# Second block's forgetting attention: VectorE evicts the projection half and makes the weights' low parts ahead of scaling the probabilities

## The chip, the cores and the metric

The kernel runs on one NeuronCore of one Trainium2 chip. The core has five engines that run side by side, each on its own list of instructions in order: TensorE (PE), VectorE (DVE), ScalarE (ACT), GpSimd (POOL) and SyncE (SP), and they wait for each other by semaphores. The metric is the time of one execution on the device in microseconds (us); the kernel before and the changed one are compared by the medians of their runs.

## The reference, cut to what matters

Two blocks of two layers each work on 512 tokens of 1024 features in float32. The change touches the attention of the second block alone, which is computed once in each of its two layers ("the two passes"):

```python
def forgetting_attention(q, k, v, logf):          # (1, 8 heads, 512, 64)
    c = jnp.cumsum(logf, axis=-1)
    for i in range(S // Q_BLOCK):                  # 4 blocks of 128 queries
        logits = einsum(q_block, k[:q1]) * HEAD_DIM_2 ** -0.5
        logits = logits + (c[q0:q1, None] - c[None, :q1])
        p = softmax(where(causal, logits, -inf))
        outs.append(einsum(p, v[:q1]))
```

In the same layer the input is projected by a wide matrix (`h @ w_in[l]`) to queries, keys, values, convolution inputs, pooling input and gates, most of which the attention doesn't need. After the attention come the convolution, pooling and gated merge, an output projection and a gated feed-forward part.

## The kernel before, in words

**Projections.** Weights arrive from HBM in units of 128x2048 float32. The matmuls want them as two rounded parts: ACT writes the high part (`split` in the scalar block: `wH<-raw`, L1298), DVE subtracts it from the raw unit and writes the low part (`split` in the vector block: `wL<-raw,wH`, L1755). Each product is then three passes over the array (L472). There are two buffers for units. A job is one group of matmuls into one of two slots of the PSUM tensor `G`. DVE frees the slot by reading it out (an eviction), and counts that in `job_free`; PE starts a job only when the one two before it was freed.

**The attention loop.** 8 heads by 4 query blocks give 32 rows; two rows (one query block of a pair of heads) are a step d, with d from 0 to 15, and the row's width is 128, 256, 384 or 512 keys in turn. Every engine has the same loop over d written out by hand in its own block of the program, so the order of each engine is the order of its code:

- PE (L1175 to L1212), step d: scores of rows 2d and 2d+1 into `psS` (L1157), a quarter of a projection unit (`fill(2d)`), the transposes of rows 2d-2 and 2d-1 into `psT` (L1193; they wait for `p_ready`), a second quarter (`fill(2d+1)`), and from step 2 on the product of two rows' probabilities with the values (L1166, `pv_pair`). `fill(13)`, in step 6, ends with sums of squares of the queries (L531, 16 small matmuls) which go into the PSUM bank `G[:, 1, :]`. That bank also holds the first finished attention output, so L531 waits for `pv_free`, which DVE's first `heads_out` counts.
- ACT (L1692 to L1706), step d: the exponential of rows 2d and 2d+1 (L1405, `p_exp`), the copies of the transposed rows 2d-2 and 2d-1 (L1411), in steps 6, 10 and 14 its half of `heads_out` (L1689), and in `fill(2d)` of every even step the high part of a weight unit (L1298). In step 14 it also rounds the pooling branch (L1682, L1683).
- DVE (L2680 to L2698), step d: scale and mask the scores and take the row maximum, for rows 2d and 2d+1 (`row`: L2556, L2559, L1997); then the reciprocal of the sums (L2690) and the scaling of the probabilities (L2691, which counts `p_ready`); in steps 6, 10 and 14 `heads_out` (L2639, which counts `pv_free`); then `fill(2d)`, which evicts the half job of the step before (L2578, L2580, L2587, L2593, in two steps after L2598 for the keys) and in every even step makes the low part of a unit (L1755); then `fill(2d+1)`, which holds pieces of the pooling branch (L2648 to L2668).

The rows' probabilities lie in four buffers by row number, the sums and reciprocals in four columns.

Of the kernel before, what the change touches and what calls it, by code (L numbers as in the profile page):

```python
# [211 lines left out]
def program(nc, a, out, scratch):  # L212
    ctx = contextlib.ExitStack()
    with ctx:
# [1532 lines left out]
        def _(dve):  # L1747
# [3 lines left out]
            def split():  # L1751

                g = c.unit
                dve.wait_ge(wh_ready, g.v + 1)
                V.tensor_tensor(wL[:, g.p, :], raw[:, g.p, :], wH[:, g.p, :].bitcast(F32), ALU.subtract)\  # L1755
                    .then_inc(wl_ready, 1)
                g.off += 1
# [87 lines left out]
            def rstd_part(at):  # L1845

                c.sq.off += 1
                dve.wait_ge(sq_used, c.sq.v)
                over = rb2[:, 0:8].unsqueeze(1).to_broadcast([P, 2, 8])
                c.link(V.tensor_tensor(ms[:, 0:16].rearrange("p (n c) -> p n c", n=2),  # L1850
                                       at[:, 0:16].rearrange("p (n c) -> p n c", n=2), over, ALU.mult))
                V.tensor_scalar(ms[:, 0:16], ms[:, 0:16], 1.0 / 64, EPS, ALU.mult, ALU.add).then_inc(ms_ready, 1)
                c.stat.off += 1

            def rstd_part_scaled(dst):

                dve.wait_ge(rs_ready, c.stat.v)
                d = dst.rearrange("p (n c) -> p n c", n=2)
                c.link(V.tensor_tensor(d, d, rbc[:, 0:8].unsqueeze(1).to_broadcast([P, 2, 8]), ALU.mult))
# [27 lines left out]
            def column_pairs(first):  # L1887

                wait(dve, rb_ready, c.bc.v - 1)
                V.tensor_copy(wide[:, c.bc.p, :].rearrange("p (n c) -> p n c", c=64),  # L1890
                              rsb[:, first:first + 8].unsqueeze(2).to_broadcast([P, 8, 64])).then_inc(cols_ready, 1)
                c.bc.off += 1
# [103 lines left out]
            def row_max(r, src):  # L1996
                return V.tensor_reduce(mxt[:, r % 4:r % 4 + 1], src, AX.X, ALU.max, negate=True)  # L1997
# [140 lines left out]
            for l in range(2):  # L2138
                if l == 0:
# [165 lines left out]
                    for lev in range(7):  # L2305
                        for h in range(4):
# [7 lines left out]
                            if lev < 6:  # L2314
                                if lev == 0:
                                    b = psS[:, n % 2, :].rearrange("p (k q) -> p k q", q=P)
                                    d = ws[:, DD + h, :].rearrange("p (k q) -> p k q", q=P)
                                    ins = V.tensor_tensor(d, b, hmask[:, 0:1, :].to_broadcast([P, 4, P]), ALU.mult)
                                else:
# [4 lines left out]
                                    d = later(ws[:, DD + h, :].rearrange("p (k q) -> p k q", q=P))  # L2324
# [15 lines left out]
                else:  # L2340
# [30 lines left out]
                    def row(r):  # L2371
                        h, qt = r // ST, r % ST
                        c.link(V.scalar_tensor_tensor(probs(r), psS[:, r % 2, 0:(qt + 1) * P], rsq[:, r:r + 1],
                                                      ws[:, OE + h, (3 - qt) * P:S], ALU.mult, ALU.add))
                        row_max(r, probs(r)).then_inc(mx_ready, 1)
# [137 lines left out]
            for l in c.layers(2, chain=CHAIN_2, **LAYER):  # L2513
# [56 lines left out]
                def half_raw(t, dst, mul=None):  # L2570

                    if t == 0:
                        dve.wait_ge(act_read, c.ar.v + 1)
                        c.ar.off += 1
                    else:
                        dve.wait_ge(sq_ready, c.sq.v + 1)
                    if mul is None:
                        half(lambda g: V.tensor_copy(dst, g), unit=(t == 1))  # L2578
                    else:
                        half(lambda g: V.tensor_scalar(dst, g, mul, None, ALU.mult), unit=(t == 1))  # L2580

                def half_values(t):

                    def read(g):
                        for i in range(2):
                            tt = 2 * t + i
                            ins = V.tensor_scalar(ws[:, FV + tt, 256:512], g[:, i * 256:i * 256 + 256],  # L2587
                                                  rbc[:, tt * 2:tt * 2 + 1], None, ALU.mult)
                        return ins
                    half(read, unit=(t == 1))  # L2590

                def half_scaled(t, dst):
                    half(lambda g: V.tensor_tensor(ws[:, dst + t, :], g, rbt, ALU.mult), unit=(t == 1))  # L2593

                def half_keys(t):
                    k_ = ws[:, FK + 2 + t, :]
                    dve.wait_ge(rb_ready, c.bc.v)
                    V.tensor_tensor(k_, k_, G[:, 3, :], ALU.mult).then_inc(kn_read, 1)  # L2598

                def fill(s_):  # L2600

                    if s_ == 2:
                        half_raw(0, ws[:, FK + 2, :])
                    elif s_ == 4:
                        half_raw(1, ws[:, FK + 3, :])
                    elif s_ == 6:
                        rstd_part(G[:, 3, :])
                        half_raw(0, ws[:, FQ + 2, :], gqk[:, 5:6])
                    elif s_ == 8:
                        rstd_part_scaled(rsb[:, 0:16])  # L2610
                        column_pairs(0)
                        half_raw(1, ws[:, FQ + 3, :], gqk[:, 5:6])
                    elif s_ == 10:
                        half_keys(0)
                        half_scaled(0, PX_)
                        column_pairs(8)
                    elif s_ == 12:
                        half_keys(1)
                        half_scaled(1, PX_)
                    elif s_ == 15:  # L2620
                        rstd_part_scaled(rsq[:, 16:32])
                    elif s_ in (17, 19, 21, 23, 25, 27):
                        pooled((s_ - 17) // 2)
                    elif s_ in (14, 16):
                        half_values((s_ - 14) // 2)
                    elif s_ in (18, 20):
                        half_scaled((s_ - 18) // 2, CX)
                    elif s_ in (22, 24):
                        half_scaled((s_ - 22) // 2, CB)
                    elif s_ in (26, 28):  # L2630
                        half_scaled((s_ - 26) // 2, CC)
                    elif s_ in (30, 32, 34, 36):
                        n = (s_ - 30) // 2
                        half_scaled(n % 2, GATE + n // 2 * 2)
# [16 lines left out]
                def pooled(n):  # L2651

                    if n == 0:
                        dve.wait_ge(pinv_in, (c.lay.v - 2) * 16)
                        window(pa, u, 1)
                    elif n == 1:
                        window(pb, pa, 2)
                    elif n == 2:
                        window(pa[:, 1:2, :], pb[:, 1:2, :], 4)
                    elif n == 3:  # L2660
                        window(pb[:, 1:2, :], pa[:, 1:2, :], 8)
                    else:
                        t, rows, widths = ((pa, lo, (2, 8)), (pb, hi, (4, 16)))[n - 4]
                        start = t[rows, :, 0:16]
                        c.link(V.tensor_tensor(start, start, ws[rows, PINV:PINV + 2, 0:16], ALU.mult))
                        V.tensor_tensor(start, start, u[rows, :, 0:16], ALU.subtract)
                        for i, width in enumerate(widths):
                            ins = V.scalar_tensor_tensor(t[rows, i, 16:S], t[rows, i, 16:S], 1.0 / width, u[rows, i, 16:S],  # L2668
                                                         ALU.mult, ALU.subtract)
                        ins.then_inc(pd_ready, 1)  # L2670
# [9 lines left out]
                for d in range(16 + 3):  # L2680
                    if d == 7:
                        rstd_part(G[:, 1, :])
                    if d < 16:
                        for r in (2 * d, 2 * d + 1):
                            dve.wait_ge(s_done, c.row.v + (r + 1))
                            row(r)
                    if d < 16:
                        for r in (2 * d, 2 * d + 1):
                            dve.wait_ge(p_exp, c.row.v + (r + 1))
                            c.link(V.reciprocal(rden[:, r % 4:r % 4 + 1], den[:, r % 4:r % 4 + 1]))  # L2690
                            V.tensor_scalar(probs(r), probs(r), rden[:, r % 4:r % 4 + 1], None, ALU.mult)\  # L2691
                                .then_inc(p_ready, 1)
                    if d in (6, 10, 14):
                        heads_out((d - 6) // 4)
                    fill(2 * d)
                    if d == 0:
                        split()
                    fill(2 * d + 1)  # L2698
                heads_out(3)
# [266 lines left out]
```

## Time and profile before

| | us |
|---|---|
| median of 3 runs (lowest to highest) | 3091.82 (3090.43 to 3093.57) |
| the profiled execution | 3094.84 |
| its span, first to last instruction | 3093.1 |
| PE busy in the span | 3076.0 (99%) |
| DVE, ACT, POOL busy | 1568.6 (51%), 1091.7 (35%), 236.9 (8%) |
| first pass of the attention loop | 1665.90 to 1806.30 |
| second pass | 2399.00 to 2540.00 |

The span is what the instructions cover; the profiled execution has 1.7 us around it. "Busy" counts an engine's instructions as they overlap on it. In a timeline the times are us from the start of the span, and the brackets at the end of a row give how long the engine sat idle before the instruction and which instruction released it. PE overlaps its matmuls, so that two of them that lie 0.23 us apart each show some 0.39 us.

### The profile page before, as it was taken

To read this page: it belongs to the slowest core of one execution; us is meant where nothing else is said; L and a number is where in the kernel's file an instruction comes from. 1 tells how busy PE (TensorE), PEld (TensorE's weight loads), DVE (VectorE), ACT (ScalarE), POOL (GpSimd) and SP (SyncE) were. 2 spreads that over 40 slices of the span, in tenths; PEclk is the share of its full clock that TensorE was granted. 3 is DMA by queue.
4 is the path that set the end of the run, shared out by engine and by line. 5 is a ranking of instruction groups with operands and counts; after the bars stand their busy time and mean duration, and the time that the engine had idled before them with its cause. 6 is when DMAs were issued, how large, how long until landed. Compare 5 with 4: busy or idle time off the path is not lost.

```text
span 3093.1 us, 36907 instructions
## 1 busy us (share of the span) xinstructions
PE 3076.0 (99%) x15434; PEld 2577.6 (83%) x15434; DVE 1568.6 (51%) x1887; ACT 1091.7 (35%) x1175; POOL 236.9 (8%) x138
## 2 busy tenths in 40 slices
PE   9999999999999999999999999999999999999999
PEld 8798988888889798888888778888888878888887
DVE  7564555554335654555436764544334766443432
ACT  3223344443223433444323332334322342333321
POOL 0002100010000010001001000101100000100100
PEclk9999999999999999999999999999999999999999
DMA  4412312223322131222333122222233223223222
GB/s 172 116 55 82 136 55 95 95 95 109 113 105 96 55 137 55 96 107 83 109 109 103 69 96 96 96 95 95 95 109 115 74 79 106 87 94 108 89 102 95
DMA packets 47758, 299.82 MB, mean 97 GB/s; under 512 B 7107, under 2 KB 7395, under 8 KB 13460
## 3 DMA queue, kind: packets, MB, share of 16 engines
q1 hardware_dynamic: 43376, 285.94, 26.2%
q10 hardware_dynamic: 4260, 12.10, 1.6%
q8 instruction: 95, 1.56, 0.2%
q14 instruction: 27, 0.22, 0.0%
HBM read 293.26 MB, written 4.77 MB: 96 GB/s over the span
## 4 chain that ended last, share of the span: by engine, by line
PE 93%; DVE 4%; ACT 2%; issue 1%; POOL 0%; DMA 0%; SPq 0%; DVEq 0%; ACTq 0%
PE G L472 86%; DVE wL L1755 1%; PE psS L830 1%; DVE mxt L1997 1%; ACT wH L1298 1%; PE psS L528 1%; PE psS L1029 1%; PE psS L1157 1%; PE G L1166 0%; PE G L1036 0%; PE G L991 0%; DVE ws L2556 0%; PE psT L1193 0%; PE psS L961 0%; PE psT L560 0%
## 5 line engine op out<-in xcount | busy, mean ns | idle before, releaser
L472 PE MATMUL G<-hH,wH 128*128 128x512 f32 x2560 | 1015.9, 397 | 6.5 <-DVE ws L2593 1.9
L472 PE MATMUL G<-hH,wL 128*128 128x512 f32 x2560 | 999.6, 390 | 0.0
L472 PE MATMUL G<-hL,wH 128*128 128x512 f32 x2560 | 998.5, 390 | 0.0
L1755 DVE TENSOR_TENSOR wL<-raw,wH 128x2048 fp32r<-128x2048 f32 x258 | 621.9, 2410 | 485.5 <-ACT wH L1298 485.4
L1298 ACT ACTIVATE wH<-raw 128x2048 fp32r<-128x2048 f32 x261 | 498.8, 1911 | 775.5 <-PE G L472 757.5
L472 PE MATMUL G<-wsr,wH 128*128 128x512 f32 (+1 forms) x2496 | 739.3, 380 | 2.4 <-DVE wsr L2389 1.9
L472 PEld LDWEIGHTS G<-hH,wH 128*128 128x128 f32 x2560 | 481.9, 188 | 119.2 <-issue 18.7
L472 PEld LDWEIGHTS G<-hH,wL 128*128 128x128 f32 x2560 | 481.4, 188 | 102.1
L472 PEld LDWEIGHTS G<-hL,wH 128*128 128x128 f32 x2560 | 482.2, 188 | 98.6 <-issue 1.2
L472 PEld LDWEIGHTS G<-wsr,wH 128*128 128x128 f32 x2496 | 459.8, 188 | 92.7 <-DVE wsr L2389 2.8
L472 PE MATMUL G<-wsr,wL 128*128 128x512 f32 (+1 forms) x1248 | 472.5, 379 | 0.0
L472 PEld LDWEIGHTS G<-wsr,wL 128*128 128x128 f32 x1248 | 234.9, 188 | 43.5
L2815 POOL TENSOR_TENSOR wsr<-sq,wsr 128x1024 f32 x44 | 105.9, 2406 | 836.5 <-ACT wsr L1436 836.5
L1878 DVE TENSOR_TENSOR sq<-G,hmask 128x1024 f32<-128x1024 f32 x44 | 53.9, 1225 | 217.6 <-PE G L472 217.6
L1436 ACT ACTIVATE wsr<-sq 128x1024 f32 x44 | 46.7, 1060 | 309.9 <-DVE sq L2020 309.9
L1405 ACT ACTIVATE ws<-ws,mxt 128x128 f32<-128x128 f32 (+3 forms) x96 | 54.0, 563 | 188.6 <-DVE mxt L1997 188.0
L1930 DVE TENSOR_TENSOR x<-x,G 128x1024 f32<-128x1024 f32 x38 | 46.4, 1221 | 142.0 <-PE G L472 142.0
L2793 POOL TENSOR_TENSOR rsb<-ms,neghalf 128x4 f32<-128x4 f32 (+4 forms) x20 | 36.8, 1842 | 998.6 <-DVE ms L1809 859.3
L472 PE MATMUL G<-wH,hH 128*128 128x256 f32 x384 | 112.2, 292 | 0.3 <-DVE ws L2381 0.3
L472 PE MATMUL G<-wH,hL 128*128 128x256 f32 x384 | 108.6, 283 | 0.0
L472 PE MATMUL G<-wL,hH 128*128 128x256 f32 x384 | 108.6, 283 | 0.0
L1878 DVE TENSOR_TENSOR tn<-G,hmask 128x1024 f32<-128x1024 f32 x44 | 53.9, 1225 | 95.2 <-PE G L472 94.8
(306 smaller groups left out, 2533.1 us busy)
## 6 DMA issues: line engine op xcount, KB each, us to landing
raw<-in_units SPq DMA_DIRECT2D x263, 1024.0 KB, 4.8
ws<-bias_rows SPq DMA_DIRECT2D x2, 1536.0 KB, 15.2
bias_rows<-ws ACTq DMA_DIRECT2D x1, 2560.0 KB
x<-in_x SPq DMA_DIRECT2D x4, 512.0 KB, 7.6
ws<-in_mem ACTq DMA_DIRECT2D x2, 1024.0 KB, 4.7
ws<-bias_rows ACTq DMA_DIRECT2D x1, 2048.0 KB, 8.6
ws<-norm_rows ACTq DMA_DIRECT2D x1, 2048.0 KB, 7.0
out_x<-x SPq DMA_DIRECT2D x3, 512.0 KB, 7.2
```

The lines of the kernel that those rows point to most:

```text
L472: mm = pe.matmul(o, mv if swap else wt, wt if swap else mv, start=first and n == 0, stop=last and n == 2)
L528: mm = pe.matmul(st[:, col:col + 1], lhs, ones[:, 0:1], start=True, stop=True)
L830: mm = pe.matmul(psS[:, n % 2, o:o + w], k_[:, ks:ks + P], q, start=True, stop=True)
L1029: mm = pe.matmul(psS[:, r % 2, 0:M], ws[:, XQ + 2 * h + t, qt * P:qt * P + P], kx[:, 2 * h + t, :], start=(t == 0), stop=(t == 1))
L1298: activation(wH[:, g.p, :], raw[:, g.p, :], ACT.Copy).then_inc(wh_ready, 1)
L1405: return activation(p_, p_, ACT.Exp, bias=mxt[:, r % 4:r % 4 + 1], accum_out=den[:, r % 4:r % 4 + 1])
L1436: activation(aH[:, bass.ds(i * 2, 2), :], sq[:, 1], ACT.Copy).then_inc(ffn_h, 1)
L1755: V.tensor_tensor(wL[:, g.p, :], raw[:, g.p, :], wH[:, g.p, :].bitcast(F32), ALU.subtract)\
L1878: V.tensor_tensor(dst, g, rb_pair, ALU.mult).then_inc(job_free, 1)
L1930: V.tensor_tensor(x[:, 2 * jj:2 * jj + 2, :], x[:, 2 * jj:2 * jj + 2, :], g, ALU.add)\
L2793: W.tensor_tensor(dst[:, at:at + cols], ms[:, at:at + cols], neghalf[:].to_broadcast([P, cols]), ALU.pow)\
L2815: W.tensor_tensor(aL[:, bass.ds(i * 2, 2), :], sq[:, 1], aH[:, bass.ds(i * 2, 2), :].bitcast(F32), ALU.subtract).then_inc(ffn_ready, 1)
```

## The change

In each step of the attention loop but the first, DVE's `fill(2d)` now stands ahead of the scaling of the probabilities of rows 2d and 2d+1. All that `fill(2d)` does goes with it: the eviction of the half job, in the even steps the low part of a weight unit (L1755) with its wait for ACT's high part, and in steps 6 and 12 and the like whatever else that index holds. `heads_out` of steps 6, 10 and 14 stood between the two and now comes after both. Step 0 keeps its order.

```diff
@@ -2684,6 +2684,8 @@
                         for r in (2 * d, 2 * d + 1):
                             dve.wait_ge(s_done, c.row.v + (r + 1))
                             row(r)
+                    if d:
+                        fill(2 * d)
                     if d < 16:
                         for r in (2 * d, 2 * d + 1):
                             dve.wait_ge(p_exp, c.row.v + (r + 1))
@@ -2692,8 +2694,8 @@
                                 .then_inc(p_ready, 1)
                     if d in (6, 10, 14):
                         heads_out((d - 6) // 4)
-                    fill(2 * d)
                     if d == 0:
+                        fill(0)
                         split()
                     fill(2 * d + 1)
                 heads_out(3)
```

The scaling has lines 2692 and 2693 in the changed file. DVE's order in step 6, from the end of `row(13)` to the start of step 7, before (in brackets the semaphores that a row waits for):

```order
L2690 RECIPROCAL rden<-den 128x1 [waits p_exp]
L2691 TENSOR_SCALAR ws<-ws,rden 128x384 [waits dve_chain]
L2690 RECIPROCAL rden<-den 128x1 [waits p_exp]
L2691 TENSOR_SCALAR ws<-ws,rden 128x384 [waits dve_chain]
L2639 TENSOR_TENSOR wsr<-G,wsr 128x512 [waits pvh_ready,pv_done]
L2598 TENSOR_TENSOR ws<-ws,G 128x512 [waits rb_ready]
L2593 TENSOR_TENSOR ws<-G,hmask 128x512 [waits job_done]
L1755 TENSOR_TENSOR wL<-raw,wH 128x2048 [waits wh_ready]
L1850 TENSOR_TENSOR ms<-G,rb 128x16 [waits sq_used]
```

and now:

```order
L2598 TENSOR_TENSOR ws<-ws,G 128x512 [waits rb_ready]
L2593 TENSOR_TENSOR ws<-G,hmask 128x512 [waits job_done]
L1755 TENSOR_TENSOR wL<-raw,wH 128x2048 [waits wh_ready]
L2692 RECIPROCAL rden<-den 128x1 [waits p_exp]
L2693 TENSOR_SCALAR ws<-ws,rden 128x384 [waits dve_chain]
L2692 RECIPROCAL rden<-den 128x1 [waits p_exp]
L2693 TENSOR_SCALAR ws<-ws,rden 128x384 [waits dve_chain]
L2639 TENSOR_TENSOR wsr<-G,wsr 128x512 [waits pvh_ready,pv_done]
L1850 TENSOR_TENSOR ms<-G,rb 128x16 [waits sq_used]
```

`heads_out` (L2639) and the two scalings now stand behind the low part (L1755), which waits for ACT's high part. Steps 10 and 14 have the same pattern; in step 10 the half of the keys is not there and a pooling piece follows. Before:

```order
L2691 TENSOR_SCALAR ws<-ws,rden 128x384 [waits dve_chain]
L2690 RECIPROCAL rden<-den 128x1 [waits p_exp]
L2691 TENSOR_SCALAR ws<-ws,rden 128x384 [waits dve_chain]
L2639 TENSOR_TENSOR wsr<-G,wsr 128x512 [waits pvh_ready,pv_done]
L2593 TENSOR_TENSOR ws<-G,hmask 128x512 [waits job_done]
L1755 TENSOR_TENSOR wL<-raw,wH 128x2048 [waits wh_ready]
```

and now:

```order
L2593 TENSOR_TENSOR ws<-G,hmask 128x512 [waits job_done]
L1755 TENSOR_TENSOR wL<-raw,wH 128x2048 [waits wh_ready]
L2692 RECIPROCAL rden<-den 128x1 [waits p_exp]
L2693 TENSOR_SCALAR ws<-ws,rden 128x384 [waits dve_chain]
L2692 RECIPROCAL rden<-den 128x1 [waits p_exp]
L2693 TENSOR_SCALAR ws<-ws,rden 128x384 [waits dve_chain]
L2639 TENSOR_TENSOR wsr<-G,wsr 128x512 [waits pvh_ready,pv_done]
```

The orders of PE, ACT, POOL and SP are the same in both kernels.

## Rows read from the trace of the kernel before

**Rows 1.** The page: busy time by engine, share of the span, instructions.
```profile
PE 3076.0 (99%) x15434; PEld 2577.6 (83%) x15434; DVE 1568.6 (51%) x1887; ACT 1091.7 (35%) x1175; POOL 236.9 (8%) x138
```

**Rows 2.** PE's waits, whole span: us in total, times, longest us.
```profile
PE G L472 <- DVE ws L2593: 1.9, 4, 0.7
```

**Rows 3.** PE in the first pass: us, PE busy (x), PEclk, DMA share, GB/s.
```profile
1665.90:1806.30 140.40, 139.47 (x827) 1.00 0.20 72
```

**Rows 4.** Timeline of DVE, first pass, step 6: start us, us, instruction.
```profile
1715.98 0.15 DVE L2690 RECIPROCAL rden<-den 128x1 f32<-128x1 f32 x1
...
1717.04 0.42 DVE L2691 TENSOR_SCALAR ws<-ws,rden 128x384 f32<-128x384 f32 x1
1717.94 0.69 DVE L2639 TENSOR_TENSOR wsr<-G,wsr 128x512 fp32r<-128x512 f32 x1 [0.48 <-ACT wsr L1689]
1718.55 0.68 DVE L2598 TENSOR_TENSOR ws<-ws,G 128x512 f32<-128x512 f32 x1
...
1719.74 2.28 DVE L1755 TENSOR_TENSOR wL<-raw,wH 128x2048 fp32r<-128x2048 f32 x1
1721.94 0.17 DVE L1850 TENSOR_TENSOR ms<-G,rb 128x16 f32<-128x16 f32 x1
```

**Rows 5.** Timeline of ACT, high parts of steps 6, 10 and 14.
```profile
1717.72 1.92 ACT L1298 ACTIVATE wH<-raw 128x2048 fp32r<-128x2048 f32 x1
...
1750.70 1.92 ACT L1298 ACTIVATE wH<-raw 128x2048 fp32r<-128x2048 f32 x1
...
1782.22 1.92 ACT L1298 ACTIVATE wH<-raw 128x2048 fp32r<-128x2048 f32 x1
```

**Rows 6.** Timeline of PE, small matmuls of step 6, first and second pass.
```profile
1719.28 1.84 PE L531 MATMUL G<-halves,sq 128*128 128x2 f32 x16
...
2452.62 1.84 PE L531 MATMUL G<-halves,sq 128*128 128x2 f32 x16
```

**Rows 7.** Timeline of DVE, second pass, `heads_out` of step 6.
```profile
2451.28 0.69 DVE L2639 TENSOR_TENSOR wsr<-G,wsr 128x512 fp32r<-128x512 f32 x1 [0.48 <-ACT wsr L1689]
```

**Rows 8.** Timeline of DVE, first pass, steps 9 to 11.
```profile
1746.07 0.62 DVE L2556 SCALAR_TENSOR_TENSOR ws<-psS,rsq,ws 128x384 f32<-128x384 f32 x1 [0.31 <-PE psS L1157]
...
1752.65 2.29 DVE L1755 TENSOR_TENSOR wL<-raw,wH 128x2048 fp32r<-128x2048 f32 x1 [0.45 <-ACT wH L1298]
1754.87 0.68 DVE L2648 TENSOR_TENSOR sq<-sq 128x508 f32<-128x508 f32 x1
...
1755.79 0.75 DVE L2556 SCALAR_TENSOR_TENSOR ws<-psS,rsq,ws 128x512 f32<-128x512 f32 x1
...
1758.60 0.69 DVE L1997 TENSOR_REDUCE mxt<-ws 128x1 f32<-128x512 f32 x1
```

**Rows 9.** Timeline of PE, first pass, steps 5, 12, 15 and 16.
```profile
1707.46 0.38 PE L1193 MATMUL psT<-ident,ws 128*128 128x128 f32 x2
...
1760.40 0.49 PE L1157 MATMUL psS<-ws 64*128 64x128 f32 x4
...
1761.60 0.47 PE L472 MATMUL G<-hH,wH 128*128 128x512 f32 x1 [0.71 <-DVE ws L2593]
...
1787.83 0.82 PE L1193 MATMUL psT<-ident,ws 128*128 128x128 f32 x6
...
1792.20 0.47 PE L472 MATMUL G<-hH,wH 128*128 128x512 f32 x1 [0.22 <-DVE ws L2593]
```

**Rows 10.** Timeline of DVE, first pass, step 15's first row.
```profile
1786.39 0.74 DVE L2556 SCALAR_TENSOR_TENSOR ws<-psS,rsq,ws 128x512 f32<-128x512 f32 x1
```

**Rows 11.** Timeline of PE, start of the kernel.
```profile
9.76 0.50 PE L472 MATMUL G<-hH,wH 128*128 128x512 f32 x1 [1.82 <-DVE wL L2113]
...
10.32 0.59 PE L472 MATMUL G<-hH,wL 128*128 128x512 f32 x1
...
13.70 0.43 PE L472 MATMUL G<-hL,wH 128*128 128x512 f32 x1
```

**Rows 12.** PE in a window there: us, PE busy (x), PEclk, DMA share, GB/s.
```profile
11.30:13.30 2.00, 2.00 (x7) 0.50 1.06 446
```

## The prediction, made before the changed kernel ran

> **What bounds the kernel now.** I read the page first: PE is busy for 3076.0 us of the span of 3093.1 [rows 1]. So the kernel can be made faster only where PE stands still, and whatever makes PE stand still longer is added to the time in full. Next, PE's own waits: the only ones that DVE's evictions in the attention loop cause are four on L2593, 1.9 us in total [rows 2]. The first pass of the loop shows PE at granted clock 1.00, with 0.93 us of 140.40 not busy [rows 3]. That is the whole prize. Last, the timelines of the two passes, to see how late each step of DVE's could come before PE waits for it. What DVE hands to PE in the loop is p_ready (scaled rows), the row maximum with the emptied score bank, job_free (evictions), wl_ready (low parts) and, once at step 6, pv_free.
>
> **Part 1, the gain.** The four waits are two in each pass, 0.71 us in step 12 and 0.22 us in step 16 of the first [rows 9] and the same in the second. An eviction that comes earlier can end them: at most -1.9 us. In the odd steps the eviction moves ahead of two scalings, 1.1 us or less.
>
> **Part 2, heads_out of step 6.** DVE finishes row 13 at 1715.98 and then before scaled two rows, ran heads_out (L2639) from 1717.94 to 1718.63, evicted, and made the low part [rows 4]. PE's sums of squares, which wait for that heads_out, start at 1719.28 [rows 6]. So heads_out had a slack of 0.6 us. Now it stands behind L1755, and L1755 waits for ACT's high part, which runs from 1717.72 to 1719.64 [rows 5] and isn't moved by the change: ACT's exponentials, copies and its half of heads_out wait for nothing that the change delays before this point. Forward from 1715.98: L2598 and L2593 take 0.60 each from start to start, to 1717.18. L1755 starts 0.03 after the high part, 1719.67, and frees DVE 2.20 later (1719.74 to 1721.94 in rows 4), at 1721.87. The two scalings took 1.48 from 1715.98 to the end of L2691 at 1717.46; 0.25 of it was the wait for the second exponential, which is long over now, and 0.15 of the rest overlaps the next instruction or the first: 1.08 is left, to 1722.95. heads_out takes 0.69, to 1723.64. PE's matmuls, seen at 1719.28, can issue from 1719.16, when the last weights of the quarter have gone in, and now issue at 1723.67. **That is a new stall of 4.5 us.** It lies on PE's own list: scores, quarters and transposes behind it can't pass. DVE starts step 7 with L1850, which waits for just these sums, so DVE, and ACT behind its maxima, shift by the same 4.5 us and nothing is caught up. The second pass has heads_out at 2451.28 and the sums at 2452.62 [rows 6, 7], the same 1.34 us apart: another 4.5. Two passes: +9.0 us.
>
> **Part 3, the scalings behind L1755 in steps 8 to 15** (times without the shift of part 2, which all engines share). In an even step the low part is bound by ACT, so the two scalings, hidden before in DVE's wait for ACT, now follow it and delay the next row. In step 8 that is 0.8 us (128 wide); 0.21 and 0.31 us of idle time in step 9 take part of it back [rows 8], and 0.3 us reach step 10. There: high part to 1752.92 (1750.70 + 1.92 + 0.3) [rows 5], low part to 1755.15, scalings 1.08, heads_out 0.61, the pooling piece 0.92 (1754.87 to 1755.79 [rows 8]): step 11's first row starts at 1757.76 instead of 1755.79, 1.97 us late. Its last maximum ends at 1761.26 instead of 1759.29. PE wants that maximum for the scores of step 12 at 1760.40 [rows 9]: wait 0.9. The eviction behind it ends at 1761.86, and the quarter that before started at 1761.60, after its own wait of 0.71, starts at 1761.89. Net +0.3: the wait that the change aims at isn't ended but replaced. Steps 12 and 13 carry some 1.5 us of lag on to step 14, where the high part ends near 1785.64 instead of 1784.14 [rows 5], the low part at 1787.87, and the second scaling at 1788.99. PE wants it for the transposes at 1787.83 + 0.3 [rows 9]; the first row's three come first, and PE loses 0.5. heads_out follows, and step 15's rows start at 1789.6 instead of 1786.39 [rows 10], its eviction ends near 1793.7, and PE, which before started step 16's quarter at 1792.20 [rows 9], starts it 1.5 us late in all. Part 3: +1.5 a pass, +3.0 us, with part 1 already inside it. Bounds: 0 (if DVE's idle time in steps 11 to 13 takes in more than I count) and 5.0 (2.5 a pass, if every 1.97 us of lag came through at the second place as well).
>
> Before step 6 I count nothing. The lags there are 0.7 to 1.0 us by the same reckoning; the closest is step 4's scaling, which I find ready at 1706.3, where PE's transposes stand at 1707.46 [rows 9], and DVE's wait for the scores of step 6 takes the lag in. PE, ACT and SP get no instruction more. SP's loads wait for L1755, which comes no earlier and at most 2 us later for a unit needed two steps on.
>
> **Part 4, PE's clock after a stall.** The loop has no stall of 4.5 us to read from. The nearest row is the kernel's start: PE idles for 1.82 us to 9.76, and from 10.32 the matmuls stand 0.43 apart instead of 0.23, at granted clock 0.50 in 11.30 to 13.30, that is 1.2 GHz, until 13.70 [rows 11, 12]. Eight steps in 3.38 us instead of 1.82: 1.6 us lost. A hole of 4.5 us, followed by 16 matmuls of two columns, is deeper than that one, while the work before it is denser. I take the fall as likelier than not: +1.6 a pass, +3.2 us. Bounds: 0, and twice that, 6.4 us, since the low clock may hold through the sums as well. The Trainium skill, page "TensorE: Matmul & The Clock Gate", section "Why this matters for your kernels", says that gaps without work between bursts of matmuls put the array back to its lower clock. By that rule the sum is 15.2 us, without it 12.0; the trace agrees at its start, and nowhere else does it show a stall long enough.
>
> **Sum.** 9.0 + 3.0 + 3.2 = +15.2 us. Against the profiled execution, 3094.84, that is 3110.0. It lies 3.0 us above the median of the runs shown, so against the median 3091.82: **3107.0 us** (+0.49%).
>
> **Rivals.** (a) The clock stays at 1.00 through both stalls: +12.0, 3103.8. For it speaks the dense work ahead of the stall, against it rows 11 and 12. (b) The low clock lasts longer, or falls again with the smaller stalls: 9.0 + 3.0 + 6.4 = 18.4, 3110.2. (c) Part 2 holds alone and DVE's idle time takes in the rest: +9.0, 3100.8. (d) Faster: the earlier evictions end the four waits and nothing takes their place, -1.9, 3089.9. The mechanism needs step 6's heads_out done by 1719.16, so ACT's high part would have to be done 4.5 us earlier than at 1719.64, before ACT's copies are; the trace shows nothing that moves it. The Trainium skill, page "Perfetto Trace Analysis", section "Optimization Strategy", advises to find the gaps of the busiest engine and to make what they wait for start sooner. That is this rival; it would give 3089.9, and rows 4 to 6 speak against it because the same move makes a tighter dependency start later. (e) The change does nothing: evictions and scalings swap places and every consumer has slack, 3091.8. It falls by the same 0.6 us of slack.
>
> **Chances.** Forecast 0.55, (a) 0.25, (b) 0.10, (c) 0.05, (e) 0.03, (d) 0.02. A measurement of this kernel can tell about 0.2% (6.2 us) from no change. Forecast and (a) to (c) all lie above 3098.0: slower 0.95, same 0.03, faster 0.02. The range takes in (c) to (b), with the bound of 5.0 of part 3: 3100 to 3112.
>
> **What would show it.** PE's waits after: a new one before L531 of some 4.5 us in each pass, released by DVE's L2639; waits of 0.2 to 1 us before L1157 in step 12 and L1193 in step 15; in step 6, L1755 idle for some 2.5 us before its start and L2693 behind it; the clock below 1.00 in the windows right behind the two stalls. Wrong would be: L531 waiting less than 3 us (another order of ACT's), the passes longer than 149 us (something else late, such as a weight unit), or time added outside the two passes.

## The result, and the profile after

The changed kernel takes 3113.3 us (median of 6 runs, 3110.31 to 3114.28) against 3093.4 us for the kernel before in the same comparison (6 runs, 3090.43 to 3095.32): ratio 1.0062, 95% interval 1.0052 to 1.0072, that is 19 us slower (16 to 22); the two medians lie 19.9 us apart. Forecast were 3107.0 us (+15.2) and a range that ended at 3112. The direction was right, the size was 4.7 us short, and another 1.6 us come from the kernel before, whose median is 3093.4 in this comparison and was 3091.8 in the runs that the forecast started from.

PE's waits in the stretch of the whole span (same view as [rows 2]: us in total, times, longest us):

```profile
PE G L531 <- DVE wsr L2639: 8.5, 2, 4.2
PE G L472 <- DVE ws L2593: 2.0, 4, 0.8
...
PE psS L1157 <- DVE mxt L1997: 1.5, 2, 0.7
...
PE psT L1193 <- DVE ws L2693: 0.6, 2, 0.3
```

The first line is new: two stalls ahead of the sums of squares, released by `heads_out`. The second is the line that the change aims at; in sum it is as large as before, but split in another way: in the first pass step 12's wait fell from 0.71 to 0.20 us and step 16's rose from 0.22 to 0.82 (step 16 is the loop's turn behind the last rows). The third and fourth are new too, the late maxima of step 11 and the late scaling of step 14.

DVE in step 6 of the first pass (it answers to [rows 4]; everything up to here lies 4.4 us earlier than in the profile of before, see below):

```profile
1711.58 0.68 DVE L2598 TENSOR_TENSOR ws<-ws,G 128x512 f32<-128x512 f32 x1
1712.18 0.69 DVE L2593 TENSOR_TENSOR ws<-G,hmask 128x512 f32<-128x512 f32 x1
1715.28 2.29 DVE L1755 TENSOR_TENSOR wL<-raw,wH 128x2048 fp32r<-128x2048 f32 x1 [2.41 <-ACT wH L1298]
1717.49 0.15 DVE L2692 RECIPROCAL rden<-den 128x1 f32<-128x1 f32 x1
...
1718.54 0.68 DVE L2639 TENSOR_TENSOR wsr<-G,wsr 128x512 fp32r<-128x512 f32 x1
1722.89 0.17 DVE L1850 TENSOR_TENSOR ms<-G,rb 128x16 f32<-128x16 f32 x1 [3.67 <-PE G L531]
```

DVE now sits idle for 2.41 us ahead of the low part, with `heads_out` behind it on its own list, and then for 3.67 us while PE does what `heads_out` released. ACT's high part was where it had been (1713.32 to 1715.24, with the same 4.4 us).

PE in the same step, and its granted clock there (second fence: us, PE busy (x), PEclk, DMA share, GB/s), which answer to [rows 6] and [rows 3]:

```profile
1719.28 3.58 PE L531 MATMUL G<-halves,sq 128*128 128x2 f32 x16 [4.24 <-DVE wsr L2639]
1722.78 0.69 PE L1166 MATMUL G<-ws 128*64 128x128 f32 x4
1723.41 2.08 PE L1157 MATMUL psS<-ws 64*128 64x512 f32 x4
```

```profile
1715.00:1719.20 4.20, 0.04 (x1) 0.75 0.17 31
1719.20:1722.60 3.40, 3.32 (x16) 0.50 0.67 275
1722.60:1726.00 3.40, 3.40 (x12) 0.50 0.00 0
1726.00:1729.00 3.00, 3.00 (x22) 0.77 0.00 0
1729.00:1733.00 4.00, 4.00 (x36) 1.00 0.00 0
```

The same 16 matmuls took 1.84 us before [rows 6] and take 3.58, and the four scores behind them take 2.08 instead of 1.13. The clock fell to 0.50 (1.2 GHz) while PE stood still, and was back at 1.00 only some 8 us after it had resumed.

**Where the time went.** One pass, from the first scores (L1157) to the last product with the values (L1166), took 139.27 and 139.31 us before, from start to start, and takes 148.87 and 149.37. Cut at three instructions that both traces show:

| stretch | first pass, us before and after | difference | second pass, difference |
|---|---|---|---|
| step 0's scores to step 6's scores | 46.21, 46.04 | -0.17 | -0.15 |
| step 6's scores to L531 | 7.13, 11.53 | +4.40 | +4.40 |
| L531 to step 7's transposes | 6.17, 9.96 | +3.79 | +4.28 |
| step 7's transposes to the end | 79.76, 81.34 | +1.58 | +1.53 |
| sum | | +9.60 | +10.06 |

The 0.15 us that both passes gain in the first stretch are won in step 5, where the 4 matmuls of L560 start earlier. The two passes together are 19.7 us longer, which is nearly all of the 19.9 between the medians. The profiled execution of the changed kernel, 3110.31 us, is the shortest of its six runs, and only 15.5 above the profile of before. The rest lies ahead of the attention loop, which begins at 1661.71 in it and at 1665.94 before: in the profile of before the clock fell several times for a few us at places the change doesn't touch, the start [rows 12] among them, and here less often. At the start:

```profile
11.30:13.30 2.00, 2.00 (x11) 1.00 1.05 438
```

Such falls are there in one profile and not in another. PE waits 1.9 us on L2389 in both kernels, to 1020.27 us before and to 1017.58 after; the clock fell there before (first line) and not after (second line):

```profile
1018.00:1026.00 8.00, 6.11 (x32) 0.79 0.47 152
1018.00:1026.00 8.00, 8.00 (x51) 1.00 0.69 257
```

I read the steps of 1.5 to 3 us between runs of one kernel as such falls. The granted clocks of the runs fit: of e11's eleven runs below, the five of 3089.7 to 3090.0 us have a mean of 0.999, the six of 3091.5 to 3093.0 one of 0.998. So the passes' lengths are the sharper measure of the stalls below, beside the medians; but each is read from one execution, and the loss to the clock within a pass can differ from one to the next as well.

### The profile page after: what moved, and what is told of

The parts are those of the page before. It is cut to its first block, busy times and chain, and to the rows that moved or that the text cites. A ratio compares the mean times of both kernels' runs of the same rounds, so it can differ in the third digit from the quotient of the medians.

```text
span 3108.5 us, 36907 instructions
## 1 busy us (share of the span) xinstructions
PE 3080.6 (99%) x15434; PEld 2578.6 (83%) x15434; DVE 1565.1 (50%) x1887; ACT 1092.1 (35%) x1175; POOL 237.7 (8%) x138
## 4 chain that ended last, share of the span: by engine, by line
PE 91%; DVE 6%; ACT 2%; issue 1%; POOL 0%; DMA 0%; SPq 0%; DVEq 0%; ACTq 0%
PE G L472 84%; DVE wL L1755 1%; ACT wH L1298 1%; DVE mxt L1997 1%; PE psS L830 1%; PE psS L1029 1%; DVE ws L2556 1%; PE psS L528 1%; PE psS L1157 0%; PE G L1036 0%; PE G L991 0%; PE G L1166 0%; PE psT L560 0%; PE psS L961 0%; PE G L531 0%
## 5 line engine op out<-in xcount | busy, mean ns | idle before, releaser
L1755 DVE TENSOR_TENSOR wL<-raw,wH 128x2048 fp32r<-128x2048 f32 x258 | 621.9, 2411 | 500.6 <-ACT wH L1298 500.5
```

## The experiments

Eleven runs of ten kernels. "Over before" is the difference of the medians in the same comparison; "passes" are the two lengths as above, less those of before.

| run | over before, us | ratio (95% interval) | passes, us |
|---|---|---|---|
| e1, heads_out first | +0.5 | 1.0000 (0.9991 to 1.0010) | +0.2, +0.2 |
| e2, low part last | -1.8 | 0.9996 (0.9986 to 1.0005) | -1.1, -1.2 |
| e3, step 6 alone | +15.6 | 1.0050 (1.0033 to 1.0067) | +9.1, +8.3 |
| e4, all but step 6 | +2.6 | 1.0010 (1.0001 to 1.0020) | +1.4, +1.4 |
| e5, 2 repeats | +1.1 | 1.0004 (0.9995 to 1.0014) | +0.4, +0.3 |
| e6, 4 repeats | +8.5 | 1.0029 (1.0017 to 1.0040) | +3.4, +3.3 |
| e7, 6 repeats | +15.0 | 1.0051 (1.0035 to 1.0068) | +4.8, +6.3 |
| e8, 3 repeats, wait ahead of the quarter | +12.1 | 1.0041 (1.0027 to 1.0055) | +5.5, +7.8 |
| e9, 8 repeats | +16.8 | 1.0054 (1.0039 to 1.0069) | +7.8, +7.9 |
| e10, 4 repeats, wait ahead of the quarter | +12.0 | 1.0041 (1.0026 to 1.0057) | +6.0, +6.2 |
| e11, low part last, again | -1.8 | 0.9993 (0.9984 to 1.0002) | -1.1, -1.1 |

### Which part of the change costs what (e1 to e4)

**e1.** `heads_out` back ahead of `fill(2d)`, against the changed kernel:

```diff
+                    if d in (6, 10, 14):
+                        heads_out((d - 6) // 4)
                     if d:
                         fill(2 * d)
...
-                    if d in (6, 10, 14):
-                        heads_out((d - 6) // 4)
```

> The changed kernel with heads_out moved back, to the place right behind the rows and ahead of fill(2d); the scalings stay behind fill(2d). Theory (heads_out behind the low part makes the stall before L531, 4.2 us a pass in the changed kernel, and the low clock after it, 3.8 us a pass, comes from that stall): both are gone, no wait before L531, clock 1.00 in both passes, and only the waits behind the late scalings are left, 0.6 to 1.6 us a pass: 1 to 3 us over the kernel before. Rival (the lateness of the scalings is what costs, and heads_out only shows it): still 10 us or more over the kernel before.

Measured: +0.5 us over the kernel before, no wait before L531, and of PE's waits in the two passes only these:

```profile
PE G L472 <- DVE ws L2593: 0.8, 4, 0.2
PE psT L1193 <- DVE ws L2695: 0.5, 2, 0.3
```

One line that moves takes away all but half a us of 19. The late scalings cost even less than expected. The wait for the late maxima (L1157) is gone, as it should be if `heads_out` no longer adds its 0.6 us to the lag of steps 10 and 14. The listed waits are 0.6 us less than before in sum (1.9 to 1.3), yet the passes are 0.2 us longer each. So the list doesn't hold all that a late hand-over costs: the six transposes that waited in step 15 now also take 1.07 us in place of 0.82 [rows 9].

**e2.** The evictions ahead of the scalings, but the low part behind them and behind `heads_out`, against the changed kernel (and in `half`, `late.append(1)` for `split()`):

```diff
                     if d in (6, 10, 14):
                         heads_out((d - 6) // 4)
+                    if late:
+                        split()
+                        late.pop()
```

> The changed kernel with the eviction ahead of the scalings as in the change, but the low part of the unit (L1755) behind the scalings and behind heads_out. Theory (what hurts is only the wait for ACT's high part, which stands ahead of the scalings and heads_out): no wait before L531, because heads_out ends 0.3 us later than in the kernel before against a slack of 0.5 to 0.6, and the four waits on L2593 shrink: 0 to 2 us faster than the kernel before. Rival (even the evictions, 0.6 to 1.2 us, are too much ahead of heads_out): a wait before L531 of some tenths of a us to 1 us, and if that is enough to lower the clock, 3 us or more a pass.

Measured: -1.8 us by the medians, both passes 1.15 us shorter. No wait of PE's in either pass is left, neither the four on L2593 nor one of the new kinds. About 1 us of the 1.15 lies behind step 7, where the waits were, and the rest in step 5, for which the prediction counted nothing. The first theory held. So "evict first" was sound; what spoilt it is that `fill(2d)` also holds a wait for ACT.

**e3.** The change in step 6 alone, against the changed kernel:

```diff
-                    if d:
+                    if d == 6:
                         fill(2 * d)
...
                         heads_out((d - 6) // 4)
+                    if d != 6:
+                        fill(2 * d)
                     if d == 0:
-                        fill(0)
```

> The change in step 6 alone, all other steps in the order of before. Theory (the whole cost of step 6 is stall plus low clock, and the late scalings of steps 8 to 15 are a cost of their own): wait before L531 4.2 us, low clock 3.8 us a pass, so 16.0 us over the kernel before. Rival (the low clock needs the late scalings around it, or the other steps cause part of the stall): less than 12 us over.

**e4.** The change in all steps but 6, against the changed kernel:

```diff
-                    if d:
+                    if d not in (0, 6):
                         fill(2 * d)
...
                         heads_out((d - 6) // 4)
+                    if d in (0, 6):
+                        fill(2 * d)
                     if d == 0:
-                        fill(0)
```

> The change in all steps but step 6. Theory: no wait before L531, clock 1.00 in both passes, and the waits of steps 11 to 16 cost 1.5 us a pass: 3.0 us over the kernel before. Rival (those waits are a consequence of the stall of step 6): within 1 us of the kernel before.

e3 gave +15.6 us with 4.24 us of wait before L531 in each pass, e4 +2.6. They add up to 18.2, about the changed kernel's 19.9, and both lie where the theory put them. The clock took 4.7 us of e3's first pass and 3.9 of its second. e4's waits are the two small ones of the changed kernel (same view):

```profile
PE G L472 <- DVE ws L2593: 2.0, 4, 0.8
...
PE psS L1157 <- DVE mxt L1997: 1.5, 2, 0.7
PE psT L1193 <- DVE ws L2693: 0.6, 2, 0.3
```

So part 3 of the prediction is a cost of its own, 1.4 us a pass, and not a consequence of the stall.

### What the stall costs beyond its length (e5 to e10)

The disputed term is the clock. These kernels have DVE's order of before, with the multiplication of the eviction repeated ahead of `heads_out` of step 6. The repeats write what the eviction then writes again; nothing is left out. With n repeats (and `CHAIN_2`, the program's count of VectorE's linked instructions, raised by n):

```diff
+                    if d == 6:
+                        dve.wait_ge(job_done, c.job.v + 1)
+                        for _ in range(n):
+                            c.link(V.tensor_tensor(ws[:, PX_ + 1, :], G[:, c.job.p * 2, :], rbt, ALU.mult))
                     if d in (6, 10, 14):
                         heads_out((d - 6) // 4)
```

> The kernel before, with two repeats of the eviction's multiplication (128x512, about 0.72 us each) put ahead of heads_out of step 6; they write what the eviction writes again afterwards. heads_out is some 1.4 us later, slack 0.5 to 0.6: a wait of 0.9 us before L531 in each pass. Theory (a hole of idle time plus the small matmuls behind it must grow past some size before the clock falls): clock 1.00 in both passes, 1.8 us over the kernel before. Rival (any wait there lowers the clock): 1.6 us or more a pass on top, 5 us over.

> The same with four repeats: a wait of 2.3 us before L531. It lies between a wait of 0.9 and the 4.2 us of the changed kernel. Theory (size of the hole): the clock may fall in some passes; if it does, the loss is 1.6 to 3.8 us a pass. So 4.6 us over the kernel before without, 8 to 12 us with a fall. Rival (the low clock's loss grows with the wait in proportion, 3.8 for 4.2 us): 2.1 us a pass, 8.8 us over.

> The same with six repeats: a wait of 3.8 us before L531, with no low part, no scaling and no other move of the change. Theory (the stall makes the low clock, whatever makes the stall): the clock falls in both passes as in the changed kernel, 3.8 us a pass lost, so 15 us over the kernel before. Rival (the changed kernel's other late work matters): clock 1.00, 7.6 us over.

> The kernel before with eight repeats ahead of heads_out of step 6. The repeats so far cost 0.73 us each (waits of 1.57 with four, 3.02 with six), so a wait of 4.5 us before L531, about the changed kernel's 4.24. Theory (stall length and what follows it set the low clock, nothing else of the change does): 3.2 to 3.8 us lost to the clock in each pass, as in the changed kernel, 15 to 17 us over the kernel before. Rival (the late low part and scalings of the changed kernel made its low clock last): 1.6 us lost a pass, 12 us over.

Measured, with L531 later by so much against step 6's transposes (before: 3.30 us behind them), and the rest of the pass's growth as what the clock took (for the changed kernel, the growth between L531 and step 7's transposes):

| repeats | L531 later, us | lost to the clock, first and second pass, us |
|---|---|---|
| 2 (e5) | 0.3 | 0, 0 |
| 4 (e6) | 1.7 | 1.6, 1.5 |
| 6 (e7) | 3.2 | 1.6, 3.1 |
| 8 (e9) | 4.6 | 3.2, 3.2 |
| the change in step 6 alone (e3) | 4.4 | 4.7, 3.9 |
| the changed kernel | 4.4 | 3.8, 4.3 |

A repeat costs 0.73 us. e5's wait was far shorter than the 0.9 us expected: the slack at this place is 1.2 us and not 0.6, because the repeats also fill the 0.48 us in which `heads_out` waited for ACT [rows 4]; its rival, a fall with any wait, couldn't show itself at so short a delay.

e6: the clock fell in both passes, at the cheap end. The loss isn't in proportion to the stall (1.6 for 1.7 us, 3.2 for 4.6): with repeats it lay near 0, 1.6 or 3.2, and nowhere between. e7 lost less to the clock in its profile than I expected (3.8), and its profiled run is the shortest of its four (3104.48 to 3108.97); its median, +15.0, is what the theory gave.

e9, which copies only the stall, costs 16.8 us, as much as the changed kernel's 19.9 less its 3.1 for the late scalings, and about what e3 costs (15.6): the stall brings the low clock, whatever makes the stall. How long the clock stays low is another matter. By the traces e3 lost more a pass than e9, but both profiles are the slowest of their four runs, and by the medians e3 isn't slower than e9; so no difference between them is shown.

**e8 and e10: other work behind the stall.** Three and four repeats, and PE waits ahead of the second quarter, so that 24 dense matmuls (256 columns) come first and the small ones after:

```diff
                 def fill(s_):
+                    if s_ == 13:
+                        pe.wait_ge(pv_free, c.pv.v + 1)
                     if 12 <= s_ < 16:
```

> Three repeats, and TensorE waits for heads_out of step 6 ahead of the second quarter of step 6 (24 dense matmuls of 256 columns, 2.9 us), not ahead of L531: a stall of 4.4 us like the changed kernel's 4.2, but dense matmuls follow it. Theory (the 16 matmuls of two columns and the small ones behind them keep the clock low after the stall): the clock is back to 1.00 within 4 us after the stall, the low clock costs 1.7 us or less a pass, 12 us or less over the kernel before. Rival (the stall's length alone sets how long the clock is low): about 8 us of low clock after the stall, 3.8 us a pass, 16 us over.

> Four repeats, and TensorE waits for heads_out ahead of the second quarter of step 6: a stall of 4.4 us, as long as the one of eight repeats, with 24 dense matmuls behind it and the 16 small ones after those. Theory (small matmuls right behind the stall keep the clock low): less is lost than with eight repeats, 1.6 to 2.5 us a pass, 12 to 14 us over the kernel before. Rival (only the stall's length counts): the same as eight repeats, 15 to 17 us over.

e8 didn't tell the theories apart: after a stall of 3.7 us, not the 4.4 expected, its first pass lost some 1.5 us and its second some 3.8. e9 and e10 have stalls of the same length. PE and its clock in e9's first pass:

```profile
1725.87 3.02 PE L531 MATMUL G<-halves,sq 128*128 128x2 f32 x16 [4.48 <-DVE wsr L2639]
```

```profile
1726.00:1729.50 3.50, 3.50 (x22) 0.57 0.02 5
1729.50:1733.00 3.50, 3.50 (x13) 0.50 0.73 262
```

and in e10's:

```profile
1719.76 0.58 PE L472 MATMUL G<-wH,hH 128*128 128x256 f32 x1 [4.44 <-DVE wsr L2641]
1724.03 1.84 PE L531 MATMUL G<-halves,sq 128*128 128x2 f32 x16
```

```profile
1719.00:1722.50 3.50, 2.74 (x13) 0.54 0.00 0
1722.50:1726.00 3.50, 3.50 (x33) 0.97 0.48 154
```

With dense matmuls first the clock is back at some 1722.7, 3 us after the stall, and the 16 small ones run at full speed (1.84 us). With the small ones first it is still at 0.50 in the window that ends 7 us after the stall. Some 1.3 and 1.5 us are lost in e10's passes, 3.2 in each of e9's. The medians differ by 4.7 us the same way, and the slowest of e10's four runs (3108.15) is faster than the fastest of e9's four (3109.42). I take it as shown that what follows the stall matters.

It is not the whole: e8's second pass shows that dense work first doesn't always bound the loss, and why the changed kernel loses 3.8 and 4.3 where e9 loses 3.2 stays open. The moment of the fall doesn't settle it. In the changed kernel the clock fell in the middle of the stall (0.75 as the mean of 1715.00 to 1719.20), in e9's first pass some 0.6 us after its end. But in e3's first pass it was still at 1.00 late in the stall, which ended at 1724.18, and then stayed low longest, for the greatest loss of all:

```profile
1720.20:1724.00 3.80, 0.00 (x0) 1.00 0.13 26
1724.20:1734.20 10.00, 10.00 (x42) 0.50 0.24 95
```

**e11.** e2 again, with more rounds.

> The variant with only the eviction ahead and the low part last, again, with more rounds. Theory (the four waits of 1.9 us in all are gone and nothing took their place): 1.9 us faster than the kernel before, ratio 0.9994. Rival (the gain of 1.8 us seen in the medians is scatter of clock falls elsewhere in the program): ratio 1.0000, 0 us.

-1.8 us again (3091.51 against 3093.35), and no wait of PE's on L2593 in the trace. The interval still takes in 1.0000, so from the medians alone this is no proven gain. The two runs agree, and so do the traces: both passes are 1.15 us shorter in e2 and in e11. It is the best of the versions that ran.

## Why the prediction was right and wrong

**What bounds the kernel, and the prize (part 1).** Right. What moved are PE's waits and, behind them, its clock. The prize was 1.9 us; e2 collected it (passes 2.3 us shorter in sum, medians 1.8). In the changed kernel it wasn't collected (L2593: 2.0 us).

**Part 2, heads_out of step 6.** Right in mechanism and size: 4.5 us of stall a pass forecast, L531 later by 4.40 in both; the idle time ahead of L1755 was forecast as some 2.5 and is 2.41. e1 and e3 show that it is this place and this instruction.

**Part 3, the late scalings.** Right: 1.5 us a pass forecast, 1.58 and 1.53 measured, 1.4 in e4 where it stands alone. The waits are the forecast ones: 0.74 us before step 12's scores and 0.29 before step 15's transposes.

**Part 4, the clock.** That it would fall was right. The step that failed is its price, 1.6 us a pass where 3.8 and 4.3 were lost: 8.1 us instead of 3.2 in all, more than the bound of 6.4 I had set. The price was taken from the one fall at the kernel's start [rows 11, 12], where a stall of 1.82 us is followed by matmuls of 512 columns. Here the stall is longer, the clock falls while it lasts, and 16 matmuls of two columns and the small products and scores follow it, all at half speed. e6, with a stall of 1.6 us, costs just the 1.6 us a pass of that row; e9 costs 3.2, e10 with dense work first 1.3 to 1.5. So the row was a fair price for a stall of its own kind and not for this one, and twice the row was no upper bound either. The prediction took the start as the nearest row, and overlooked one that is nearer in kind: in the trace of before another stall has small matmuls on both sides. PE waited 0.73 us between two groups of 16 matmuls of one column; the second group took 3.17 us where the first took 1.84, and the clock stayed low for nearly 7 us (PE's timeline, then its windows, in the kernel before):

```profile
253.08 1.84 PE L528 MATMUL psS<-ones,sq 128*128 128x1 f32 x16
255.65 3.17 PE L528 MATMUL psS<-ones,sq 128*128 128x1 f32 x16 [0.73 <-ACT sq L1323]
```

```profile
256.00:258.00 2.00, 2.00 (x12) 0.53 0.00 0
258.00:260.00 2.00, 2.00 (x7) 0.50 0.00 0
260.00:263.00 3.00, 3.00 (x8) 0.51 0.03 5
```

Half of that time is lost, an estimate of some 3.4 us from these windows; at that price for each pass the sum is 18.8 us.

One sign that the prediction named for being wrong came true: passes longer than 149 us. By the bounds of [rows 3] they are 149.96 and 150.46, against 140.4 before. The cause was not the one named there, a late weight unit, but the low clock.

With part 4 at the measured 8.1 the sum is 9.0 + 3.0 + 8.1 = 20.1, against 19.9 measured. The count of nothing before step 6 was off by 0.15 us a pass.

**The rivals.** (a), the clock stays up, is refuted by the windows. (c) is refuted by e4, and (e) and (d) by the result. (d)'s advice is right for e2, where the low part isn't in the way. (b), more low clock than one fall, is what came, with a price set too low (18.4 us in all) and a chance of 0.10. The rule of the Trainium skill, page "TensorE: Matmul & The Clock Gate", section "Why this matters for your kernels", that gaps between bursts of matmuls bring the lower clock, agrees with the trace after (0.50 in 1719.20 to 1726.00). The page "Perfetto Trace Analysis", section "Optimizing Scalar/DVE Operations", of the Trainium skill says that where VectorE isn't saturated but makes bubbles on other engines, breaking instructions up may let work finish sooner. No run here breaks up an instruction. e2 does the like with a block: it takes `fill(2d)` apart and puts the part that PE waits for first (-1.8 us).

## What to carry to other kernels

Before a block of work is moved ahead on an in-order engine, list every wait inside it: a block that contains a wait for another engine moves everything behind it to that engine's pace, and the tightest hand-over behind it (here 0.6 to 1.2 us of slack) sets the price. Move only the part that has no such wait. And where TensorE will stand still, price the stall as its length plus the lower clock that may follow, and look at what comes next on its list: here a stall of 4.5 us cost 3.2 us more a pass with small matmuls right behind it and 1.3 to 1.5 more with dense ones. A delay of 0.3 us cost nothing more in e5, but 0.73 us between groups of one-column matmuls did in the kernel before.

## What the runs showed of the hardware that I had not expected

- The loss to the lower clock doesn't grow evenly with the stall: 0 us for a delay of 0.3, 1.6 for 1.7, 1.6 or 3.1 for 3.2, 3.2 for 4.6, and 3.8 to 4.7 for 4.4 in the changed kernel and e3. In one kernel it differs between two equal passes (e3, e7, e8).
- The clock can fall during the stall (mean 0.75 in 1715.00 to 1719.20), so that the first 8 us behind it run at half speed: the 16 matmuls of two columns took 3.58 us instead of 1.84.
- The same wait doesn't always bring the clock down: after 1.9 us on L2389 it fell in the profile of before and stayed at 1.00 in the one after. Two profiles of nearly equal kernels differ by 4 us ahead of the changed place in this way, and I read the steps of 1.5 to 3 us between runs of one kernel the same way.
